# The first four key-weight units of a two-block transformer kernel, loaded behind the memory and the constants

## What is computed

```python
def ada_params(cond, w, b):
    mod = jax.nn.silu(cond) @ w + b
    return jnp.split(mod, 3, axis=-1)

xm_l = x_lat * (1.0 + sc_l) + sh_l
xm_c = x_ctx * (1.0 + sc_c) + sh_c
```

```python
def rmsnorm(x, w):
    xf = x.astype(jnp.float32)
    y = xf * lax.rsqrt(jnp.mean(xf * xf, axis=-1, keepdims=True) + NORM_EPS)
    return (y * w.astype(jnp.float32)).astype(x.dtype)

mem_n = rmsnorm(mem, norm_mem_w[l])
k = (mem_n @ w_k).reshape(b, m, XA_HEADS, XA_HEAD_DIM)
```

## Time and profile before

| | us |
|---|---|
| median of three runs | 3252.22 |
| lowest, highest | 3250.27, 3253.8 |
| the profiled execution, its own time | 3254.03 |
| its span, first to last instruction | 3252.2 |
| TensorE busy (matmuls) | 3118.1, 96% of the span |
| VectorE busy | 2257.0, 69% |
| ScalarE busy | 1620.2, 50% |
| bytes moved by DMA | 666.43 MB, mean 205 GB/s |

### The profile page before, as it was taken

How to read it: one execution, slowest core, us unless ns; L and a number is a source line. 1 busy time by engine, 2 the same in 40 slices (tenths; PEclk the granted TensorE clock), 3 DMA queues, 4 the chain that set the end, 5 groups by cost and what they waited for, 6 DMA issues and landing times.

```text
span 3252.2 us, 45074 instructions
## 1 busy us (share of the span) xinstructions
PE 3118.1 (96%) x16882; PEld 2675.4 (82%) x16882; DVE 2257.0 (69%) x2760; ACT 1620.2 (50%) x1942; POOL 56.6 (2%) x52
## 2 busy tenths in 40 slices
PE   6998989999799998999999999999999999999997
PEld 5887877888688886788888888888888888888886
DVE  6878776778658877654766875466557777777554
ACT  5754442455443556454455655445435555555442
POOL 0003300000000000000000000000000000000000
PEclk8999999999899998999999999999999999999999
DMA  7976682877467864555555555556445555555553
GB/s 274 359 268 238 214 295 77 304 277 278 139 202 266 290 209 153 193 189 183 163 189 177 172 187 192 188 183 238 144 139 184 189 181 190 196 181 195 189 190 124
DMA packets 179817, 666.43 MB, mean 205 GB/s; under 512 B 20036, under 2 KB 20420, under 8 KB 178248
## 3 DMA queue, kind: packets, MB, share of 16 engines
q1 hardware_dynamic: 177992, 660.09, 60.0%
q10 hardware_dynamic: 1664, 4.19, 0.3%
HBM read 657.91 MB, written 6.29 MB: 204 GB/s over the span
## 4 chain that ended last, share of the span: by engine, by line
PE 82%; DVE 10%; ACT 3%; DMA 2%; issue 1%; DVEq 1%; ACTq 0%; SPq 0%
PE acc L740 44%; PE acc L744 22%; DVE w_lo L1859 4%; PE acc L751 3%; PE acc L752 3%; PE acc L753 3%; ACT w_hi L1231 1%; DVE mod_raw L1870 1%; DMA ada_raw<-in_w_ada 1%; DMA mod_raw<-in_w_mod 1%; DMA raw<-in_w_mix_out 0%; PE msc L851 0%; PE acc L903 0%; PE msc L1131 0%; PE msc L1151 0%
## 5 line engine op out<-in xcount | busy, mean ns | idle before, releaser
L1859 DVE TENSOR_TENSOR w_lo<-raw,w_hi 128x1024 fp32r<-128x1024 f32 x1020 | 1242.2, 1228 | 607.8 <-ACT w_hi L1231 598.1
L1231 ACT CAST w_hi<-raw 128x1024 fp32r<-128x1024 f32 x1020 | 1060.9, 1048 | 817.8 <-PE acc L744 594.5
L740 PE MATMUL acc<-a_pair,w_hi 128*128 128x512 f32 x2944 | 932.4, 398 | 8.3 <-DVE w_lo L1859 5.7
L744 PEld LDWEIGHTS acc<-a_pair,w_lo 128*128 128x128 f32 x2944 | 554.8, 188 | 131.3
L740 PE MATMUL acc<-b_pair,w_hi 128*128 128x512 f32 x1792 | 572.4, 401 | 11.4 <-DVE w_lo L1859 6.3
L744 PE MATMUL acc<-a_pair,w_lo 128*128 128x256 f32 x2944 | 580.0, 278 | 0.0
L740 PEld LDWEIGHTS acc<-a_pair,w_hi 128*128 128x128 f32 x2944 | 451.6, 189 | 11.4 <-issue 3.9
L740 PE MATMUL acc<-f_pair,w_hi 128*128 128x512 f32 x1408 | 442.4, 395 | 0.0
L744 PEld LDWEIGHTS acc<-b_pair,w_lo 128*128 128x128 f32 x1792 | 339.7, 190 | 80.5
L744 PE MATMUL acc<-b_pair,w_lo 128*128 128x256 f32 x1792 | 354.6, 279 | 0.0
L744 PEld LDWEIGHTS acc<-f_pair,w_lo 128*128 128x128 f32 x1408 | 264.5, 188 | 62.5
(11 more groups left out here) (353 smaller groups left out, 2807.4 us busy)
## 6 DMA issues: line engine op xcount, KB each, us to landing
raw<-in_w_ffn_up SPq DMA_DIRECT2D x176, 512.0 KB, 4.0
mod_raw<-in_w_mod SPq DMA_DIRECT2D x128, 512.0 KB, 5.1
raw<-in_w_ffn_down SPq DMA_DIRECT2D x88, 512.0 KB, 3.3
ada_raw<-in_w_ada SPq DMA_DIRECT2D x64, 512.0 KB, 5.6
raw<-in_w_xa_k SPq DMA_DIRECT2D x32, 512.0 KB, 6.6
raw<-in_w_k SPq DMA_DIRECT2D x32, 512.0 KB, 3.7
raw<-in_w_v SPq DMA_DIRECT2D x32, 512.0 KB, 5.3
raw<-in_w_even_out SPq DMA_DIRECT2D x32, 512.0 KB, 4.8
```

Source lines behind the costliest of these rows:

```text
L740: pe.matmul(acc[:, bank(stage, g) + m, :], w_h[:, cols], pair[:, :, kc, :], start=begin, stop=False, skip_group_check=True)
L744: mm = pe.matmul(acc[:, bank(stage, g) + m, 0:T], w_l[:, cols], pair[:, 0, kc, :], start=False, stop=end, skip_group_check=True)
L1231: nc.scalar.copy(w_hi[:, slot], source).then_inc(hi_done, 1)
L1859: vec.tensor_tensor(w_lo[:, slot], source, w_hi[:, slot].bitcast(F32), ALU.subtract).then_inc(lo_done, 1)
```

## The change

```diff
@@ load_first
                 for j, (kind, g, k, _) in enumerate(stage.kinds):
                     if stage.name == "mem_k" and j == ADA_RING:
                         load_mem()
+                        for n in range(RING):
+                            nc.sync.dma_start(raw[:, n].rearrange("p a b -> p (a b)"), t[stage.weights][n]).then_inc(raw_landed[n], 16)
                     if j == 24:
 
                         sp.wait_ge(pe_step, AFTER["mem_norm"]["pe"])
                         nc.sync.dma_start(x[:], t["ctx"]).then_inc(ctx_in, 16)
                     n = PLACE[kind].index((stage.name, j))
+                    if kind == "w" and n < RING:
+                        continue
                     if n >= RING:
 
                         sp.wait_ge(lo_done, RING + UNIT_OF[kind][n - RING] + 1)
```

## The result

| | before | after |
|---|---|---|
| median of 18 runs, us | 3253.30 | 3259.53 |
| lowest to highest | 3250.27 to 3259.47 | 3254.45 to 3267.09 |
| ratio after to before, 95% interval | | 1.0017 (1.0010 to 1.0024) |
| span of the profiled execution | 3252.2 | 3252.8 |
| its mean granted clock | 0.981 | 0.983 |

The change costs 0.17%, about 5.5 us on 3253.3. Its profiled execution is one of the shortest of the 18, only 0.6 us longer than the profiled one of before. So the span of this one trace is not the result; the trace is read for where time went, place by place.

The account below looks back on a forecast made before the run. The prediction took TensorE, in a matmul for 96% of the span, as the bound, with DMA full to about 20 us. Terms 3.1 + 1.7 + 0 + 0 = +4.8 us on 3252.2 gave 3257.0 us; range 3251.0 to 3260.5.

Parts of the forecast that it names:

- Term 1: Start of the first stage: four key units ahead of a4 make its cast 5.2 us later, at 22.4 us.
- Term 2: TensorE before the second quarter's sums: idle from 21.4 to about 24.5 us, +3.1 us after 2.2 in hand.
- Term 3: Second quarter's sums on TensorE run at the low clock after the new idle time: +1.7 us, ends 0 and +2.7.
- Term 4: Queue between 21.81 and 57 us: the four transfers gone from there gain 0, at the low end 0.5 us.
- Term 5: Everything after the fourth quarter's sums moves along as one piece; nothing is taken back or added, 0.
- The allowance of +-1.4 us: First key units, 35 to 45 us: a shifted clock pattern could win or lose +-1.4 us; 0 was taken.
- The sum: Whole kernel: 3.1 + 1.7 + 0 + 0 = +4.8 us, a forecast median of 3257.0 us.
- Room in the queue that gives the time back: Rival, 80 to 120 us: 2.1 MB less backlog brings later units 5.2 us forward; -0.4, 3251.8 us; chance 8%.
- The clock did not stay up: Rival: clock stays up over the new idle time before the second sums; +3.1, 3255.3 us; chance 18%.
- The constants were on time: Rival: constants come late too, moving TensorE's start at 16.12 by up to 5.2 us; 3257.4 us; chance 9%.
- The long low clock: Rival: clock stays low through three quarters' sums and three units to 37 us; +7.5 on 3.1, 3262.8 us; chance 7%.
- The fixed 2 us of each transfer: Reading for the four moved loads, paid one after another: delay estimated 12.8 us, 3264.6 us; chance 1%.

Follow-up runs that it names:

- eight units: The changed kernel with four further unused 512 KB loads ahead of a4, eight in all; ratio 1.0030 to the kernel before.
- two units: Half of the change: only k0 and k1 ahead of a4, k2 and k3 at their old places; ratio 1.0007 to the kernel before.
- the pause was filled: The changed kernel with 14 added, unneeded TensorE matmuls between a2 and the second quarter's sums; ratio 1.0014 to the kernel before.
- the other 2 MB: The kernel before with four unused 512 KB loads ahead of a4, key units at their old places; ratio 1.0015 to the kernel before.
- the interleaved order: The kernel before with its first loads queued in order of first use; 3251.22 us against 3255.49, ratio 0.9988.
- the eight kernels: The changed kernel and the seven follow-up kernels, each timed against the kernel before; ratios from 0.9988 to 1.0030.
- removing only part of the wait: The kernel before with ident, ones and pick behind the memory's first quarter and the parameters (0.43 MB) behind a7; ratio 0.9999.
- the key units behind a7: k0 to k3 loaded early, but behind a7 instead of ahead of a4; ratio 1.0000 to the kernel before.

## Why the prediction was right

The forecast was 3257.0 us, or +4.8; the median was 3259.53 and the ratio gives +5.5. Step by step:

- **Term 1**, a4 5.2 us later: 22.52 against the 22.4 forecast, 5.3 us, and 10.3 for eight units. Right. That it is the cause is shown by two experiments together: the same loads behind a7 cost nothing, and other loads at the same place cost the same. The four loads delayed a4, which stood behind them, and not the constants, which stood ahead.
- **Term 2**, +3.1 us with 2.2 in hand: the second sums started at 24.58, the forecast was 24.5; with two units the 2.2 in hand showed as second sums only 0.2 late, at an a4 that was 2.3 late. Right.
- **Term 3**, +1.7 for the clock: the sums and a3 together brought the root to +4.96, so 1.8 in the changed kernel; and 1.6 came back when the pause was filled. Right in size and in cause, but not in its parts. The forecast had the second sums wholly at the low clock (+1.7) and a3 at the high one. In fact the clock fell some way into the sums (+1.1) and was still low in a3 (+0.65). That the two add up to the forecast is partly luck, for the term is not a constant: with the other 2 MB it was 2.5 us and with eight units 2.8 (the shift at the root less that of the second sums' start), where the low clock lasted over the sums and most of a3, near the +2.7 that stood as the upper end.
- **Term 4**, 0 for the places that were left: the other 2 MB, which left them as they were, cost 1.0015 against 1.0017. So 0 within the some 2 us that the two intervals leave.
- **Term 5**, everything else moves along: +4.96 at the root and +5.68 at the fifth copy; +10.99 there with eight units and -4.93 with the interleaved order. The allowance of +-1.4 us for the clock's later pattern was needed: shifts at the fifth copy differed from those at the root by -0.5 to +1.7 us over the eight kernels.
- **The sum** was 0.7 us under what the ratio gives, and the median 2.5 us over the forecast. The second number holds an offset that is not the change's: before, measured again, had 3253.3 instead of 3252.2.
- **The rivals.** Room in the queue that gives the time back did not happen, in either direction of shift. The clock did not stay up, though it did so for the pause itself. The constants were on time, at 16.16. The long low clock did not come. The fixed 2 us of each transfer that the Trainium skill gives for another issuing path ("DMA: Bandwidth & Descriptors", "Anatomy of one DMA — SWDGE (gpsimd) path"), paid one after another, would have put a4 at an estimated 30.0 us; it was cast at 22.52, so these loads did not pay such a time one after another. The rate in that section of the Trainium skill alone gave an estimated 4.8 us for four units, where the trace has 5.3.

I had expected a shift in the profiled span, 3257.0; it was 3252.8. What was missed there is not a term but the size of an execution's own scatter, for which I had taken the +-1.8 us of three runs. Eighteen runs spread over 9 us before and over 13 after.

## What to carry to other kernels

A queue that is full at the start of a program is a list of due dates: put each first load where its consumer needs it, and a load that nobody waits for behind all that somebody does, however free its buffer is. Before moving a load ahead, read who waits for the one that it passes, and how long: here 5.76 us of idle time on ACT said that the next transfer was already due, and 2.2 us in hand on TensorE was all the cover there was. In the other direction, ordering by first use gave about 4 us where removing only part of the wait gave nothing that the runs resolve.

## What the hardware showed beyond the forecast

The time of an execution goes with TensorE's mean granted clock. In the 18 runs of the changed kernel:

| mean granted clock | runs | us |
|---|---|---|
| 0.983 | 4 | 3254.45 to 3256.63 |
| 0.982 | 4 | 3257.38 to 3259.92 |
| 0.981 | 6 | 3258.88 to 3261.13 |
| 0.980 | 2 | 3262.99 and 3263.94 |
| 0.979 | 2 | 3261.54 and 3267.09 |

Single places where the clock was down (175 us and 2410 us in one execution of before) are there in one execution and absent in another, at 1.5 us each. The same instructions at the very start met a different clock, too, but here the row of the clock misleads. With two units ahead it says this from 16 to 21 us, where before it said 0.50:

```profile
16.00:21.00 5.00, 4.49 (x12) 3.25 (x11) 0.40 (x1) 1.48 (x2) 0.00 (x0) 1.00 1.03 415
```

TensorE's timeline of the same execution:

```profile
15.71 3.78 PE L794 MATMUL msc<-x,ones 128*128 128x256 f32 x8 [4.56 <-DMA pick<-in_pick]
18.93 0.87 PE L702 MATMUL msc<-w_hi,cond_pair 128*128 128x512 f32 x1
```

The first sums took 18.93 - 15.71 = 3.22 us, as long as before (19.34 - 16.12), so they ran at the low clock although the row has 1.00. The row shows 1.00 throughout up to 36 us in this execution, so it missed the low stretch at the start. Where a row of the clock and the durations disagree, the durations decide. They say that the clock rose while a2 ran, near 19.5 us, where before it rose near 21.4; that is the difference of about a microsecond that made TensorE early with two units ahead and with the key units behind a7.

So a difference of under about 5 us between two kernels can't be read from one profiled execution of each. It can be read from the marks inside the stage that was changed, to the 1 or 2 us that the clock moves them, and from many timed runs.
